# A time mixer's small fp32 products made split f32r products, with affines and state scalings moved from VectorE to ScalarE

## The reference, cut to what matters

```
p = h @ w_in;  pf = p + (token_shift(p) - p) * mu_shift
r, k, v, wl, al, gl = split(pf)              # 2048, 2048, 2048, 96, 96, 256 columns
decay = exp(-DECAY_SCALE * sigmoid(w0 + tanh(wl) @ w_w2))
a     = sigmoid(a0 + al @ w_a2)
g     = sigmoid(gl) @ w_g2                   # three low-rank products (w_g2 has 256 rows)
kk = k * k_k;  kk = kk / norm(kk per head)   # a sum over the 64 columns of a head
k  = k * (1 + (a - 1) * k_a)                 # an affine of a, then a product
for t:  S = S * w_t + (S @ -kk_t) (kk_t * a_t)^T + v_t k_t^T;   y_t = S @ r_t
y  = (y - mean) * rsqrt(var + eps) * gn_g + gn_b      # per head: a sum of squares
y  = (y + sum(r * k * r_k per head) * v) * g          # per head: a third sum
```

## Time and profile before

| | |
|---|---|
| time, median of 3 runs | 2407.47 us (2406.66 to 2407.55) |
| profiled execution, first to last instruction | 2404.5 us |
| its busy time on PE | 2157.6 us (90%) |
| on DVE | 1529.0 us (64%) |
| on ACT | 684.3 us (28%) |
| granted PE clock, mean | 0.992 of full speed |

### The profile page before, as it was taken

How to read it: one execution, slowest core, us unless ns; L and a number is a source line. 1 busy time by engine, 2 the same in 40 slices (tenths; PEclk the granted TensorE clock), 3 DMA queues, 4 the chain that set the end, 5 groups by cost and what they waited for, 6 DMA issues and landing times.

```text
span 2404.5 us, 37848 instructions
## 1 busy us (share of the span) xinstructions
PE 2157.6 (90%) x15331; PEld 1510.5 (63%) x15331; DVE 1529.0 (64%) x2605; ACT 684.3 (28%) x1366; POOL 659.7 (27%) x539
## 2 busy tenths in 40 slices
PE   9999999999999999998999889978877787777776
PEld 8999999999899999987554444433332233222222
DVE  7778888888765455548876567667446444444445
ACT  6555555455344444432121111111011000000000
POOL 1000000000000000004554555555455445444442
PEclk9999999999999999999999999999999999999999
DMA  6533333333367666679999999999999999999997
GB/s 213 141 95 98 102 88 101 103 88 98 106 184 194 185 187 187 190 270 342 417 427 424 425 423 426 427 427 426 427 427 428 426 427 427 427 427 427 427 427 289
DMA packets 348320, 708.19 MB, mean 295 GB/s; under 512 B 13834, under 2 KB 272482, under 8 KB 281826
## 3 DMA queue, kind: packets, MB, share of 16 engines
q0 software_dynamic: 74176, 537.01, 53.1%
q1 hardware_dynamic: 273732, 168.55, 24.1%
q10 hardware_dynamic: 240, 0.22, 0.0%
HBM read 703.63 MB, written 2.10 MB: 294 GB/s over the span
## 4 chain that ended last, share of the span: by engine, by line
DMA 36%; PE 17%; issue 2%; DVE 2%; POOL 1%; DVEq 0%; ACT 0%; POOLq 0%; ACTq 0%
DMA query_w<-in_v_table,experts 17%; DMA rows<-in_v_table,experts 13%; PE bank L1980 7%; PE project L1980 4%; DMA rows<-in_u_table,experts 3%; DMA up_rows<-in_u_table,experts 3%; PE bank L247 2%; DMA down_row_more<-in_v_table,experts 2%; PE bank L1896 2%; PE project L247 1%; PE bank L1938 0%; PE bank L1944 0%; PE bank L1612 0%; PE bank L1923 0%; POOL rows L1851 0%
## 5 line engine op out<-in xcount | busy, mean ns | idle before, releaser
L2102 DVE CUSTOM_DVE_ANT_0 rows<-rows,h 128x2048 f32<-128x2048 f32 x170 | 388.7, 2292 | 329.7 <-DMA rows<-in_u_table,experts 329.5
L1851 POOL DMA_INDIRECT rows<-in_u_table,experts x170 | 182.9, 1076 | 1097.7 <-DVE experts L1449 1040.0
L232 DVE TENSOR_TENSOR w_half_rest<-w_half,w_half_high 128x1024 fp32r<-128x1024 f32 x224 | 271.4, 1219 | 160.5 <-ACT w_half_high L211 160.3
L247 PE MATMUL project<-hT_high,w_half_high 128*128 128x272 f32 (+1 forms) x1152 | 351.1, 305 | 0.4 <-PEq L254 0.3
L1980 PE MATMUL bank<-query_w,merged_spare 128*128 128x512 f32 x608 | 283.6, 602 | 60.7 <-DMA query_w<-in_v_table,experts 47.3
L1980 PE MATMUL bank<-rows,merged_spare 128*128 128x512 f32 x612 | 286.4, 605 | 57.2 <-DMA rows<-in_v_table,experts 43.8
L247 PE MATMUL project<-hT,w_half_high 128*128 128x272 f32 (+1 forms) x1152 | 329.2, 286 | 0.0
L247 PE MATMUL project<-hT_high,w_half_rest 128*128 128x272 f32 (+1 forms) x1152 | 328.7, 285 | 0.0
L2102 DVE CUSTOM_DVE_ANT_0 up_rows<-up_rows,h 128x2048 f32<-128x2048 f32 x86 | 197.0, 2292 | 168.7 <-DMA up_rows<-in_u_table,experts 168.7
L211 ACT CAST w_half_high<-w_half 128x1024 fp32r<-128x1024 f32 x224 | 234.9, 1051 | 204.3 <-PE merge_ps L247 120.6
L1980 PEld LDWEIGHTS bank<-rows,merged_spare 128*128 128x128 f32 x612 | 114.0, 192 | 223.2 <-issue 127.3
(11 more groups left out here) (435 smaller groups left out, 3760.3 us busy)
## 6 DMA issues: line engine op xcount, KB each, us to landing
w_half<-in_w_in SPq DMA_DIRECT2D x176, 512.0 KB, 4.1
w_half<-in_w_branch_a SPq DMA_DIRECT2D x32, 512.0 KB, 3.9
out_w<-in_w_out SPq DMA_DIRECT2D x16, 1024.0 KB, 5.6
w_half<-in_w_branch_b SPq DMA_DIRECT2D x16, 512.0 KB, 3.9
query_w<-in_w_q_peer SPq DMA_DIRECT2D x8, 1024.0 KB, 16.2
out_w<-in_w_q_peer SPq DMA_DIRECT2D x6, 1024.0 KB, 19.1
lora_weights<-in_w_in SPq DMA_DIRECT2D x4, 896.0 KB, 14.1
rows<-in_u_table,experts POOLq DMA_INDIRECT x170, 21.1
```

The lines of the kernel that those rows point to most:

```text
L232: return eng.tensor_tensor(low.bitcast(F32R), x, high, ALU.subtract)
L247: mm = nc.tensor.matmul(out, a.bitcast(F32R), b.bitcast(F32R), start=start and n == 0, stop=stop and n == 2)
L1851: pool.indirect_dma_start(ur[n % RU], None, w["u_table"][0], bass.IndirectOffsetOnAxis(ap=k.idx[:, t, h, j:j + 1], axis=0)).then_inc(s_u[n ...
L2102: v.tensor_tensor_reduce(ur[n % RU], ur[n % RU], k.h[:, n // (HEADS * TOPK), :], 1.0, 0.0, ALU.mult, ALU.add, dots(n, n + 1)).then_inc(s_d ...
```

## The change

The four low-rank products become products of split operands (three f32r matmuls each, twelve for the four), and the three sums become two f32r matmuls each, of the rounded operand and of its remainder by a rounded matrix of ones. For that the weights of a pair (512 columns) and once the low-rank inputs are rounded on ACT and subtracted on DVE (`lr`); the square of k is made twice on ACT, once rounded, and subtracted on DVE (`kq`); likewise the product of r and k (`bk`, `br`) and the square of y (`yc`, `gq`). PE waits for the DVE subtraction where it waited for the operand or, in `lw`, for the transfer.

From DVE to ACT go the affine of the decay (now behind the tanh in `lw`), that of the rate (`lt`), the scaling of the state by the chunk decay (behind the copy of rhs in `r_`) and the copy of the chunk decays (`en`). The copies of a pair's vectors are dropped; the instructions read them in place from `k.vec`. The loads of low-rank weights move, in SP's queue, from behind the sixth half of a block to between its second and third, and wait for `lr` of the pair before on DVE.

```diff
 PE_ORDER
-    ... ("t", 0, 1), ("gv", 0, 3), ("f", 10, 0),
+    ... ("t", 0, 1), ("f", 10, 0), ("gv", 0, 3),
 ACT_ORDER
-    ("u", 2, 3), ("nm", 0, 1), ("r", 3, 3), ("u", 3, 3), ("r", 4, 3), ("split", 5, 0), ("split", 0, -1), ("e", 1, 0),
+    ("u", 2, 3), ("bk", 0, 1), ("nm", 0, 1), ("r", 3, 3), ("u", 3, 3), ("lr", 0, 0), ("r", 4, 3), ("split", 5, 0), ("split", 0, -1),
...
 SP
+        def low_rank_weights(sp, b):
+            wait(sp, q["lows"], b)
...
+                sp.dma_start(dst, src).then_inc(q["lora_w"], 16)
-                for u in range(6 if b else 0):
-                    k.load_half(sp, b * 6 + u)
-                wait(sp, q["lora_mm"], b * 3)
-                for dst, src in ((ww2[:], w["w_w2"][0][:, b * P:(b + 1) * P]), (wa2[:], w["w_a2"][0][:, b * P:(b + 1) * P]),
-                                 (wg2[:], Wg[:, :, b * P:(b + 1) * P])):
-                    sp.dma_start(dst, src).then_inc(q["lora_w"], 16)
+                for u in range(6):
+                    if u == 2:
+                        low_rank_weights(sp, b)
+                    if b:
+                        k.load_half(sp, b * 6 + u)
 PE
+            def low_rank(out, rows, j, t, start=True, stop=True):
+                return product(nc, out, (low_w_high[rows, j, :], low_w_rest[rows, j, :]), (lora_high[rows, j, t], lora_rest[rows, j, t]), start, stop)
+            def head_sums(out, high, rest):
+                nc.tensor.matmul(out, ones_high[:].bitcast(F32R), high.bitcast(F32R), start=True, stop=False)
+                return nc.tensor.matmul(out, ones_high[:].bitcast(F32R), rest.bitcast(F32R), start=False, stop=True)
-                nc.tensor.matmul(low[:, 0:T], ww2[:], k.lora[0:DECAY_LORA, 0, :], start=True, stop=True).then_inc(q["lora_mm"], 1)
+                low_rank(low[:, 0:T], slice(0, DECAY_LORA), 0, slice(0, T)).then_inc(q["lora_mm"], 1)
...
-                nc.tensor.matmul(low[:, 0:T], ones, sq[:, real], start=True, stop=True).then_inc(q["norm"], 1)
+                head_sums(low[:, 0:T], sq_high[:], sq_rest[:, real]).then_inc(q["norm"], 1)
...
 ACT
+                nc.scalar.activation(sq_high[:].bitcast(F32R), kx[par][:, real], ACT.Square, scale=k.vec[:, V_KK, p:p + 1]).then_inc(q["ksq"], 1)
+            def bk(_, p, par):
+                wait(act, q["bonus"], p)
+                wait(act, q["rk"], p + 1)
+                nc.scalar.copy(rk_high[:].bitcast(F32R), rk[:, CH:TP]).then_inc(q["rkr"], 1)
+            def lr(_, p, par):
...
+                nc.scalar.copy(low_w_high[:].bitcast(F32R), low_w[:]).then_inc(q["lowr"], 1)
+            def lt(_, p, par):
+                nc.scalar.activation(t1[:, real], am[:, real], ACT.Identity, scale=k.vec[:, V_KAH, p:p + 1],
+                                     bias=k.vec[:, V_KAC, p:p + 1]).then_inc(q["rate"], 1)
+            def en(_, p, par):
+                nc.scalar.copy(ends[par][:], pe_[:, CH - 1::CH]).then_inc(q["endc"], 1)
+                nc.scalar.activation(sg[:, real], sg[:, real], ACT.Copy, scale=0.5, bias=0.5).then_inc(q["sg"], 1)
             def r_(c, p, par):
                 nc.scalar.copy(rhs[:], rhs_ps).then_inc(q["rhsc"], 1)
+                if 0 < c < NCH - 1:
+                    wait(act, q["S"], p * 4 + c)
+                    nc.scalar.activation(spc[:], s[c % 2][:], ACT.Copy, scale=ends[par][:, c:c + 1]).then_inc(q["spc"], 1)
+                nc.scalar.activation(ysq_high[:].bitcast(F32R), y_ps, ACT.Square).then_inc(q["sqr"], 1)
 DVE
+            def gq(_, p, par):
+                wait(dve, q["sqr"], p + 1)
+                rest_bits(n, ysq_rest[:], ysq[:], ysq_high[:]).then_inc(q["ysplit"], 1)
-                n.tensor_scalar(sg[:, real], sg[:, real], 0.5, 0.5, ALU.mult, ALU.add)
-                n.tensor_scalar(t1[:, real], am[:, real], cur[par][:, V_KAH:V_KAH + 1], cur[par][:, V_KAC:V_KAC + 1], ALU.mult, ALU.add)
-                n.tensor_copy(ends[par][:], pe_[:, CH - 1::CH]).then_inc(q["endc"], 1)
-            def r_(c, p, par):
-                if 0 < c < NCH - 1:
-                    d()
-                    n.tensor_scalar(spc[:], s[c % 2][:], ends[par][:, c:c + 1], None, ALU.mult)
...
```

More of the change, by code:

```diff
@@ L684, in rwkv_stage @@
                  "rhs", "rhsc", "U", "Uc", "Snew", "S", "Yo", "Yc", "sqr", "var", "vsqrt",
-                 "done", "zero", "rst", "y", "yhigh")
+                 "done", "zero", "rst", "y", "yhigh", "lowr", "lows", "ones", "ksplit", "rkr", "rksplit", "ysplit", "sg", "rate", "exp1",
+                 "spc")
         q = {n: k.sem(f"r_{n}") for n in names}
-        n_zero = 6
+        n_zero = 7
         ones = k.const[:, C_ONES:C_ONES + P]
@@ L722, in rwkv_stage @@
         block = ctx.enter_context(nc.Block())
+        def low_rank_weights(sp, b):
+            wait(sp, q["lows"], b)
+            if b == 0:
+                sp.wait_ge(q["zero"], n_zero)
+            own = slice(b * P, (b + 1) * P)
+            for dst, src in ((low_w[0:DECAY_LORA, 0, :], w["w_w2"][0][:, own]), (low_w[0:ICL_LORA, 1, :], w["w_a2"][0][:, own]),
+                             (low_w[:, 2:4, :], Wg[:, :, own])):
+                sp.dma_start(dst, src).then_inc(q["lora_w"], 16)
         @block.sync
@@ L780, in lg @@
                 for j in range(2):
-                    mm = nc.tensor.matmul(low[:, 0:SEQ], wg2[:, j, :], k.lora[:, 2 + j, META:T], start=(j == 0), stop=(j == 1))
+                    mm = low_rank(low[:, 0:SEQ], slice(0, P), 2 + j, slice(META, T), j == 0, j == 1)
                 mm.then_inc(q["lora_mm"], 1)
@@ L785, in nm @@
                 wait(pe, q["sig"], p * 3 + 3)
-                wait(pe, q["ksq"], p + 1)
-                nc.tensor.matmul(low[:, 0:T], ones, sq[:, real], start=True, stop=True).then_inc(q["norm"], 1)
+                wait(pe, q["ones"], 1)
+                wait(pe, q["ksplit"], p + 1)
+                head_sums(low[:, 0:T], sq_high[:], sq_rest[:, real]).then_inc(q["norm"], 1)
             def bo(_, p, par):
                 wait(pe, q["nroot"], p + 1)
-                wait(pe, q["rk"], p + 1)
-                nc.tensor.matmul(low[:, 0:SEQ], ones, rk[:, CH:TP], start=True, stop=True).then_inc(q["bonus"], 1)
+                wait(pe, q["rksplit"], p + 1)
+                head_sums(low[:, 0:SEQ], rk_high[:], rk_rest[:, CH:TP]).then_inc(q["bonus"], 1)
             def gr(_, p, par):
@@ L890, in gv @@
             def gv(_, p, par):
-                wait(pe, q["sqr"], p + 1)
-                nc.tensor.matmul(var_ps, ones, ysq[:], start=True, stop=True).then_inc(q["var"], 1)
+                wait(pe, q["ysplit"], p + 1)
+                head_sums(var_ps, ysq_high[:], ysq_rest[:]).then_inc(q["var"], 1)
             schedule(PE_ORDER, {"f": f, "lw": lw, "la": la, "lg": lg, "nm": nm, "bo": bo, "gr": gr, "rb": rb, "t": t,
@@ L914, in e @@
                 wait(act, k.s_used, p * 6 + 2 * i + 2)
[L915 removed]
+                nc.scalar.activation(t[:, real], pr[(3 * p + i) % 2][:, 0:T], ACT.Copy, scale=k.vec[:, o, p:p + 1]).then_inc(q["own"], 1)
             def kn_(_, p, par):
@@ L929, in lw @@
                 wait(act, q["lora_mm"], p * 3 + 1)
-                nc.scalar.activation(sg[:, real], low[:, 0:T], ACT.Tanh, scale=0.5, bias=cur[par][:, V_W0H:V_W0H + 1]).then_inc(q["sig"], 1)
+                nc.scalar.activation(sg[:, real], low[:, 0:T], ACT.Tanh, scale=0.5, bias=k.vec[:, V_W0H, p:p + 1]).then_inc(q["sig"], 1)
+                wait(act, q["sig"], p * 3 + 1)
+                nc.scalar.activation(sg[:, real], sg[:, real], ACT.Copy, scale=0.5, bias=0.5).then_inc(q["sg"], 1)
             def la(_, p, par):
@@ L934, in la @@
                 wait(act, q["lora_mm"], p * 3 + 2)
-                nc.scalar.activation(am[:, real], low[:, 0:T], ACT.Tanh, scale=0.5, bias=cur[par][:, V_A0H:V_A0H + 1]).then_inc(q["sig"], 1)
+                nc.scalar.activation(am[:, real], low[:, 0:T], ACT.Tanh, scale=0.5, bias=k.vec[:, V_A0H, p:p + 1]).then_inc(q["sig"], 1)
             def lg(_, p, par):
@@ L1051, in lk @@
             def lk(_, p, par):
-                d()
+                wait(dve, q["rate"], p + 1)
                 n.tensor_tensor(k2[:, real], kx[par][:, real], t1[:, real], ALU.mult)
                 d()
-                n.scalar_tensor_tensor(out=rk[:, CH:TP], in0=r[par][:, CH:TP], scalar=cur[par][:, V_RK:V_RK + 1], in1=k2[:, CH:TP],
+                n.scalar_tensor_tensor(out=rk[:, CH:TP], in0=r[par][:, CH:TP], scalar=k.vec[:, V_RK, p:p + 1], in1=k2[:, CH:TP],
                                        op0=ALU.mult, op1=ALU.mult).then_inc(q["rk"], 1)
```

79 lines of the change are left out of this document (51 added, 28 removed), and 18 rows, old and new, of tables (ACT_ORDER, DVE_ORDER, PE_ORDER).

## The result

The changed kernel takes 2411.84 us in the median of 20 runs (2410.06 to 2413.94), the kernel before 2407.36 in 20 runs beside it (2405.38 to 2408.33): a ratio of 1.0020, 95% interval 1.0014 to 1.0026. It is slower by 4.5 us where 1.6 faster was forecast; the sign is wrong. The time lies near the upper end of the range, but by luck: what stretched the range so far, a longer wait at u3 and rival 2's wait of 0.6 a block, did not come. The profiled execution's span is 2411.7 us.

A forecast was written before the change was run, and what follows sets the result against it. PE was taken to bound the kernel. Steady blocks 4.6, plus block 17's 0.2, less block 1's 1.9, block 2's 0.3 and the stage end's 1.0, made 1.6 us saved: median 2405.9, range 2397.5 to 2414.

The forecast's parts named there:

- wait at u3: PE waits at u3, chunk 3's product needing ScalarE's copy of rhs: 0.6 us a block, bounds 0.27 to 1.16.
- rival 2: Chance 0.2: PE waits 0.6 us a block for the state of chunk 1, behind the finished y's rounding; 2414.3 us.
- What PE saves: Split f32r products replacing fp32 ones on PE save 0.93 us a block, in full in blocks 3 to 16.
- What DVE and SP do besides: DVE's added subtractions and SP's transfers waiting for `lr`: nothing in a steady block; 0.6 us a block without DVE's cover.
- So of 0.93 a block 0.33 is left: Blocks 3 to 16: PE's saving less the wait at u3, 14 x 0.33 = 4.6 us, between 9.2 and -3.2.
- the end of the stage: Block 18: the variance's subtraction ahead of DVE's pooling window costs 1.0 us, between 0 and 2.1.
- The delay of the last reciprocal: Block 18: the last reciprocal begins at about 674.2 instead of 672.14, 2.1 us of delay.
- The cover of 2.0: Block 18: 2.0 us between DVE's last subtraction (679.29) and PE's merge (681.28), set against the reciprocal's delay.
- Block 1: Without recurrence there, ScalarE's additions and `lr` with its subtraction lengthen PE's wait for B_st: 1.9 us lost.
- Block 2: The bonus's subtraction and `lr` stand ahead of B_st on DVE: 0.3 us lost, between 0 and 0.5.
- Rival 1: Chance 0.2: no wait at u3, so 0.93 us a block counts in full; 10.0 saved, 2397.5 us.
- The advice against the move: Skill page: multiplications and additions belong on VectorE; leaving the state scaling on DVE would take 3.1 us off the wait.

The follow-up runs named there:

- experiment 6: Changed kernel with DVE's decay and S_decayed waits earlier, r-k rounding behind U of chunk 3, k_for_norm earlier on ScalarE; 2400.57 us, ratio 0.9973 to the kernel before.
- experiment 3: Changed kernel, but ScalarE rounds the product of r and k behind U of chunk 3; 2409.73 us, ratio 1.0016 to the kernel before.
- experiment 9: Changed kernel with the scaling of the state by the chunk decays back on DVE; 2408.75 us, ratio 1.0006 to the kernel before.
- Experiment 5: Changed kernel, last pair only: variance amid the ten f units on PE, pooling window behind DVE's last weight remainder; 2410.65 us, ratio 1.0015 to the kernel before.
- experiment 4: Changed kernel, last pair only: variance ahead of the ten f units on PE, pooling window ahead of DVE's remainder; 2409.39 us, ratio 1.0013 to the kernel before.
- experiment 7: Changed kernel, but for pairs 1 and 2 DVE makes the low-rank weight remainder behind the stacked operands; 2411.46 us, ratio 1.0018 to the kernel before.

## Why the prediction was wrong, point by point

- **What PE saves** was right: 0.93 a block by the sum, 0.94 by experiment 6, where no new wait is left.
- **The wait at u3** was right in place, cause and size. From r of chunk 2 (524.69) to u3 (530.49) are 5.80 us, the length that the prediction gave ScalarE's chain; against PE's 5.24 that is 0.56, where 0.6 was taken. 1.19 - 0.75 = 0.44 of it shows between r of chunk 3 and u3; PE came 0.10 later to that r, for the next reason. The same distance is 5.50 in experiment 3, 0.30 less with the rounding that had been priced at 0.29, and 5.57 in experiment 9, 0.23 less with the scaling that had been priced at 0.22.
- **What DVE and SP do besides** was counted as nothing in a steady block, and rightly: experiment 6 keeps all of it, with one remainder moved, and a block there is shorter by all that PE saves.
- **The step that failed first** is "nothing" for the state on DVE: "So of 0.93 a block 0.33 is left" counted no cost at the three states. Each update of chunks 1 to 3 waits on three semaphores instead of one and starts 0.10 later, and r of the next chunk comes 0.93 after the state product where it was 0.83. So a block loses 0.3. (Chunk 0's update, with two waits, is late as well, but r of chunk 1 is not: 0.98 behind the product in both kernels.) 0.93 - 0.44 - 0.30 leaves 0.19; 0.05 more passes from u3 to the state product of chunk 3 (3.46, it was 3.41), and 0.13 is measured (35.33 - 35.20). The count of waits stood in the change; the trace of before shows no such wait and no bound was given for it.
- **The step that failed most** is the end of the stage: "I take 1.0, between 0 and 2.1". From the last y product (671.25) to the merge (687.11) are 15.86 us; before, 669.73 to 681.28, 11.55. The 4.3 lost are twice the upper bound, and three parts of the term were wrong.
  - The delay of the last reciprocal was taken as 2.1. It starts 5.15 behind the y product where it was 2.41, so 2.74 later. The prediction let PE form the variance as soon as DVE's remainder was there (673.05); the order, which the diff shows, puts ten f units first (675.39).
  - The cover of 2.0, from DVE's last remainder to the merge, was not there. PE needs the remainder of an earlier half, which DVE makes right behind the reciprocal: before, it was ready at 674.97 and PE used it at 675.12. So all 2.74 count.
  - The clock stood in no term. Experiment 6 has this end of the stage unchanged, with the same wait of 3.58 us, and its clock stayed at 1.00. From the end of the wait to the merge, the changed kernel and experiment 6 (columns of the earlier trace rows):

```profile
679.37:687.11 7.74, 7.42 (x48) 7.24 (x49) 4.00 (x6) 2.44 (x4) 0.00 (x0) 0.78 0.48 135
```

```profile
667.29:673.48 6.19, 5.87 (x49) 5.69 (x49) 4.01 (x6) 2.46 (x4) 0.00 (x0) 1.00 0.59 169
```

7.74 - 6.19 = 1.55 us for the same products, and 2.74 + 1.55 is the whole loss. Experiment 5 gives 2.5 of it back, 1.55 of that by the clock that stayed up; experiment 4 gives 1.8. Both move the variance and the pooling window at once, so what each of the two is worth by itself is not shown.
- **Block 1** was right in size (1.9 taken, 2.06 measured); experiment 7 gives 1.07 back by moving DVE's remainder of the weights, and with it the wait for ScalarE's rounding, which had been priced at 0.7 and 0.5. Block 2 (0.3, 0.46) agrees as well.
- **Rival 2**, a wait at the state behind the finished y, was right on the place and wrong on the cause. ScalarE's rounding of y did come later and DVE waited 0.56 for it, but the state of chunk 1 is late by 0.10 like those of chunks 2 and 3, where no such rounding stands ahead, and experiment 6 leaves the order there and has 0.50. Its 0.6 a block did not appear. **Rival 1** (no wait at u3) falls.
- **The advice against the move.** The Trainium skill, "ScalarE: Activation LUTs", section "Rules for kernel authors", gives multiplications and additions to VectorE. Experiment 9 agrees for the scaling: a block is 0.44 shorter. But the speed of the instruction did not decide it: it took 255 ns on DVE and takes 0.25 us from start to start on ScalarE. 0.23 of the 0.44 are ScalarE's stretch from rhs to rhs, and the rest goes with the waits at the states. The 2.7 us of the medians mix both with the 1.5 lost in block 1, so their nearness to 3.1 is chance. The affines were not tested by themselves.

## What to carry to other kernels

When work moves to another engine, price the semaphore that comes with it at every instruction on the path that will wait for it, and let an earlier instruction of that engine do the waiting where the value is known to be there. A faster product is worth what the next in-order chain leaves: read the distance between its two hand-overs and its slack, and put nothing into it that fits into an idle stretch elsewhere. And look at the last block by itself: a position in the order that is free when the pipeline is full can be the end of the path when it drains.
